# One logarithm for the two heads' units of a key block in a stick-breaking attention, in place of one for each

## What is computed

```python
z = einsum('bhqk', q_blk, kh) * Dh ** -0.5
mask = key_pos < q_pos
log_1m_beta = where(mask, log_sigmoid(-z), 0.0)
between = cumsum(log_1m_beta, reverse=True over keys) - log_1m_beta
weights = where(mask, exp(log_sigmoid(z) + between), 0.0)
out = weights @ v
```

## Time and profile before

| | us |
|---|---|
| median of 3 runs | 1442.71 |
| lowest and highest | 1438.63, 1443.05 |
| the profiled execution's own time | 1436.79 |
| its span, first to last instruction | 1435.1 |

### The profile page before, as it was taken

How to read it: one execution, slowest core, us unless ns; L and a number is a source line. 1 busy time by engine, 2 the same in 40 slices (tenths; PEclk the granted TensorE clock), 3 DMA queues, 4 the chain that set the end, 5 groups by cost and what they waited for, 6 DMA issues and landing times. The chain is left out here.

```text
span 1435.1 us, 27696 instructions
## 1 busy us (share of the span) xinstructions
PE 1358.9 (95%) x11020; PEld 1063.8 (74%) x11020; DVE 871.1 (61%) x1347; ACT 676.8 (47%) x1249; POOL 324.5 (23%) x434
## 2 busy tenths in 40 slices
PE   6999989999999899898999889999999999999997
PEld 5877767777777566555677678888887788888886
DVE  6244261575752465667365787776665656669865
ACT  5533241352423387878354645445443434345541
POOL 6675544542432042435101300000000000000000
PEclk9999999999999799999999999999999999999999
DMA  6555333533225330404242254445444865787952
GB/s 204 145 156 150 103 82 89 149 85 84 62 75 125 122 75 3 90 2 137 89 156 103 81 165 159 142 147 158 157 136 147 279 194 179 257 269 252 305 188 103
DMA packets 191546, 201.07 MB, mean 140 GB/s; under 512 B 36669, under 2 KB 127994, under 8 KB 191418
## 3 DMA queue, kind: packets, MB, share of 16 engines
q1 hardware_dynamic: 145132, 169.47, 37.5%
q10 hardware_dynamic: 46286, 29.84, 7.5%
HBM read 145.06 MB, written 54.20 MB: 139 GB/s over the span
## 5 line engine op out<-in xcount | busy, mean ns | idle before, releaser
L484 POOL TENSOR_TENSOR fr_wL<-fr_raw,fr_wH 128x256 fp32r<-128x256 f32 (+1 forms) x208 | 164.2, 821 | 76.6 <-PE fr_ps_F L1267 54.2
L1267 PE MATMUL fr_ps_F<-fr_hL,fr_wH 128*128 128x512 f32 (+1 forms) x416 | 167.9, 404 | 2.8 <-DVE fr_hL L804 2.4
L1267 PE MATMUL fr_ps_F<-fr_hH,fr_wH 128*128 128x512 f32 (+1 forms) x416 | 166.6, 400 | 0.0
L1267 PE MATMUL fr_ps_F<-fr_hH,fr_wL 128*128 128x512 f32 (+1 forms) x416 | 113.4, 402 | 0.0
L1267 PEld LDWEIGHTS fr_ps_F<-fr_hL,fr_wH 128*128 128x128 f32 (+1 forms) x416 | 76.6, 184 | 22.9 <-issue 3.1
L2618 PE MATMUL all_ps_b<-ro_hH,ro_slot 128*128 128x512 f32 x272 | 88.4, 391 | 3.0 <-ACT pl_p L2120 1.5
L1267 PEld LDWEIGHTS fr_ps_F<-fr_hH,fr_wL 128*128 128x128 f32 (+1 forms) x416 | 76.2, 187 | 20.0 <-issue 3.2
L1267 PEld LDWEIGHTS fr_ps_F<-fr_hH,fr_wH 128*128 128x128 f32 (+1 forms) x416 | 76.8, 185 | 18.8 <-issue 2.3
L478 POOL CAST fr_wH<-fr_raw 128x1024 fp32r<-128x1024 f32 (+1 forms) x42 | 48.5, 1155 | 160.3 <-PE fr_ps_F L1267 140.0
L2627 PE MATMUL all_ps_b<-ro_hH 128*128 128x512 f32 x312 | 75.9, 389 | 0.0
L2627 PE MATMUL all_ps_b<-ro_y 128*128 128x512 f32 x300 | 72.7, 389 | 0.5 <-DVE ro_y L2454 0.5
(11 more groups left out here) (480 smaller groups left out, 3154.9 us busy)
## 6 DMA issues: line engine op xcount, KB each, us to landing
pl_slot<-in_w_ff SPq DMA_DIRECT2D x88, 256.0 KB, 4.4
pl_slot<-second_operands SPq DMA_DIRECT2D x75, 256.0 KB, 3.7
fr_raw<-in_w_in ACTq DMA_DIRECT2D x37, 512.0 KB, 4.2
second_operands<-pl_hL SPq DMA_DIRECT2D x64, 256.0 KB, 2.0
pl_hT<-in_w_ff SPq DMA_DIRECT2D x44, 256.0 KB, 4.5
projected<-fr_stage ACTq DMA_DIRECT2D x39, 256.0 KB, 4.4
pl_hT<-second_operands SPq DMA_DIRECT2D x37, 256.0 KB, 3.8
pl_xt<-in_w_ff SPq DMA_DIRECT2D x16, 512.0 KB, 5.6
```

What stands on the lines that cost most here:

```text
L484: m = pool.tensor_tensor(wL[b][:, k:k + 2, 0:wd], raw[b][:, k:k + 2, 0:wd], wH[b][:, k:k + 2, 0:wd].bitcast(F32), ALU.subtract)
L1267: m = pe.matmul(F[b][0:wd, :], w[b][:, k, 0:wd], a[:, k, :], start=(at_ == 0), stop=(at_ == len(passes) - 1))
```

## The change

The four tiles `E0` to `E3` become one tile `E` of four slots, of the same size in all. `logs(i, u)` still takes the exponential of unit `u`. The logarithm is left out for even units; for odd units one instruction covers two adjoining slots, that of unit `u - 1` and that of `u`. Its semaphore `log` then counts pairs, and `softplus` of both units waits for the same count.

```diff
--- before.py
+++ after.py
@@ -2768,7 +2768,8 @@
         r.sb("early", [P, early.size])
         qd, kd, vp, kS, qH, qL = early.qd, early.kd, early.vp, early.kS, early.qH, early.qL
         vn = r.sb("vn", [P, TB + 1, P])
-        E = [r.sb(f"E{n}", [P, HALF]) for n in range(4)]
+        E_all = r.sb("E", [P, 4, HALF])
+        E = [E_all[:, n, :] for n in range(4)]
         SP = E
         row = [r.sb(f"row{n}", [1, HALF]) for n in range(4)]
         W = [r.sb(f"W{n}", [P, HALF]) for n in range(4)]
@@ -3337,12 +3338,15 @@
                 act.copy(ahead.hH[:, i, :], outT[:]).then_inc(s("m_high"), 1)
 
             def logs(i, u):
+                h, c, b, off, rows, first = UNITS[u]
                 act.wait_ge(s("z"), i * NU + u + 1)
                 if u >= 4 or i:
                     act.wait_ge(s("tri_mm"), i * NU + u - 3)
                 act.activation(part(E[u % 4], u), part(Z[u % NZ], u), ACT.Exp).then_inc(s("exp"), 1)
-                act.wait_ge(s("exp"), i * NU + u + 1)
-                act.activation(part(E[u % 4], u), part(E[u % 4], u), ACT.Ln, bias=1.0).then_inc(s("log"), 1)
+                if h:
+                    act.wait_ge(s("exp"), i * NU + u + 1)
+                    both = E_all[0:rows, u % 4 - 1:u % 4 + 1, off:HALF]
+                    act.activation(both, both, ACT.Ln, bias=1.0).then_inc(s("log"), 1)
 
             def units(i):
                 def weight(u):
@@ -3438,7 +3442,7 @@
 
             def units(i):
                 def softplus(u):
-                    dve.wait_ge(s("log"), i * NU + u + 1)
+                    dve.wait_ge(s("log"), (i * NU + u) // 2 + 1)
                     dve.scalar_tensor_tensor(part(SP[u % 4], u), part(E[u % 4], u), CAP, part(Z[u % NZ], u),
                                              ALU.min, ALU.max).then_inc(s("sp"), 1)
 
```

## The result

| | median us | runs | lowest, highest |
|---|---|---|---|
| before, measured beside it | 1440.13 | 5 | 1438.63, 1443.05 |
| after | 1461.75 | 5 | 1458.83, 1465.31 |

The ratio is 1.0146, with a 95% interval of 1.0122 to 1.0170: the change costs 21.6 us. I had said 1447.5 in a range of 1437 to 1457, so the direction was right and the size wrong.

A forecast was written before the change was run, and what follows sets the result against it. No engine alone was taken to bound `heads`: PE was busiest, but at 61 of 84 units ACT's own queue was the limit. Losses of 8.3 less 3.5 saved gave +4.8 us, 1447.5 us against the median 1442.7, range 1437 to 1457.

The forecast's parts named there:

- the seven steps: Steps between even weights in passes 0, 1 and 2 of `heads` said to be stretched, together +8.3 us.
- The ring over two units: Chain from one even weight through merged logarithm, softplus, POOL and PE to the next: 5.28 to 5.61 us per wide pair.
- The term of pass 2: Units 18 to 26: four wide pairs that took 16.78 us, stretched to 5.4 us a pair, +4.8 us.
- The last step of pass 0: From weight 24 to the sums of unit 26: lengthened by +1.9 us, expected to last.
- The step from pair 6/7 to the wide pair 8/9: First half of passes 0 and 1: chain of 4.79 us against 3.89 and 4.09, so +0.9 and +0.7 us.
- Elsewhere the ring has cover: Wide steps of pass 0, weights 16 to 24, and the end of pass 1: GLA work covers it, 0.25 to 0.6 us spare.
- narrow pairs have shorter rings: Pairs below 512 columns: chain shorter than for wide pairs, so no loss was counted for them.
- the third rival: Wide steps of passes 0 and 1: later softplus delays DVE's GLA pieces; +13.9 us, 1456.6 us; chance 0.13.
- The saving of 3.5 us: ACT's queue: 0.27 us less per pair, counted for 13 pairs taken as truly bound by ACT, -3.5 us.
- thin cover breaks: Eight wide steps of passes 0 and 1 grow 0.7 us each, nothing saved by ACT; 1456.6 us; chance 0.13.
- ACT's queue decides: Logarithm's delay is covered in passes 0 and 1, only ACT's saving counts: -9.5 us, 1433.2 us; chance 0.17.
- both cancel: PE absorbs the stretch of passes 0 and 1, only pass 2 pays: +1.3 us, 1444.0 us; chance 0.32.

The follow-up runs named there:

- split_first: Changed kernel with DVE's split put ahead of the softplus in even units of pass 2; 1467.13 us, one run.
- narrow_first: Kernel before with only pairs below 512 columns merged, and DVE's other work put ahead of the softplus in even narrow units; 1444.84 us, ratio 1.0040.
- merge_narrow: Kernel before with logarithms merged only for pairs below 512 columns; 1448.63 us, ratio 1.0086.
- merge_pass1: Kernel before with logarithms merged in pass 1 only; 1442.27 us, ratio 1.0028.
- after_first: Changed kernel, all pairs merged, with DVE's other work put ahead of the softplus in even narrow units; 1461.47 us, ratio 1.0153.
- both_short: Changed kernel with even units' row copy behind the logarithm on ACT and, in pass 2, DVE's split ahead of the even softplus; 1464.88 us, ratio 1.0180.
- late_two: Changed kernel with two single logarithms, the even one first, behind the odd exponential; each softplus waits for its own; 1452.16 us, ratio 1.0106.
- wait_pair: Kernel before, ACT's queue untouched, but an even unit's softplus also waits for the odd unit's logarithm; 1455.03 us, ratio 1.0126.
- late_rev: Changed kernel with two single logarithms behind the odd exponential, the odd one first, the even softplus waiting for both; 1472.14 us, ratio 1.0227.
- row_last: Changed kernel with the row copy of even units moved behind the logarithms on ACT; 1463.67 us, ratio 1.0170.

## Why the prediction was wrong

Its mechanism of the loss was right and its sum was too small: +4.8 us against +21.6 (25.3 in the trace of after). In that trace the way from 4.8 to 25.3 is: 3.0 more on the seven steps, 3.0 on the eight wide steps of passes 0 and 1 said to have cover, 2.0 on three wide steps that it left out, 8.1 on narrow pairs, 0.9 between the passes, and the 3.5 saved that didn't come.

- **The ring over two units** was right to the instruction, and its size a little small. The two bounds were 5.28 and 5.61, I took 5.4, it was 5.70. ACT's part came as added up (0.96, 0.61, 1.06), POOL's copy was 0.94, the slow value, each time; the handovers to POOL and PE took 0.13 and 0.15 where I had put 0.05 and 0.14. The term of pass 2 was +4.8 and measured 22.79 - 16.78 = **+6.0**.
- **The last step of pass 0**: +1.9, measured +2.7, at a granted clock of 0.85; split_first, with the same order there, took 5.37 us at 1.00, which is +1.9. **The step from pair 6/7 to the wide pair 8/9**: +0.9 and +0.7, measured +1.9 and +0.7. The pair in pass 2, which I left out, grew by 0.8. The seven steps came to 11.3 instead of 8.3.
- **"Elsewhere the ring has cover"** is the step that failed. The steps from weight 16 to 24 of pass 0 went from 23.43 to 25.34 us: the spare 0.25 to 0.6 us wasn't there, since the ring is 5.7 and the four steps aren't equal (6.30, 6.10, 5.84, 5.19). In split_first, at a granted clock of 1.00, the same four took 24.6 us, so 1.2 of the 1.9 are not the clock. Above all, **"narrow pairs have shorter rings"** compared them with the wide ring, not with their own steps. The pair of 390 columns has a ring of 4.94 us where the step was 3.15. The narrow pairs pay 8.1 us in the trace of after, and 10.8 when merged alone; narrow_first shows that about half of it or more comes with the DVE work behind the softplus, part of it queued, part of it beside POOL's copy. I had named this queue, in the third rival, but for wide pairs only.
- **The saving of 3.5 us** isn't to be seen. ACT is 7.7 us less busy, but no group of steps became shorter by more than 0.1 us (single steps of pass 1 moved by -1.0 to +1.7 us). merge_narrow, where I expected at best -2 us, and merge_pass1 are both slower. That a weight's sums were done doesn't show that ACT's queue sets the end. No run here shortens ACT's work without delaying a logarithm, so whether there is anything to save stays open.
- **The rival "thin cover breaks"** was nearest (1456.6, still 5 us short). Its eight steps (weight 16 to 24 of passes 0 and 1) grew by 3.0 us in all, not 5.6, and one of them alone, in pass 1, by 1.7; more came from narrow pairs. "ACT's queue decides" and "both cancel" are refuted by pass 2 alone, +11.3 us at a granted clock of 1.00. The page of the Trainium skill cited for the fixed cost, "VectorE: DVE Perf Modes", section "The TRN2 errata", would have given -7.9 us, an estimate from its figure; ACT's busy time did fall by 7.7, so its figure holds for the engine, and the kernel became 21.6 us slower.
- What was to show it came: wide steps of 5.70 (just above the 5.3 to 5.6 said), ACT idle for 1.4 to 1.6 us before even weights, both waits grown, `back` unchanged. One sign of being wrong came too: three of the eight wide steps of passes 0 and 1 grew by over 0.5 us (1.1, 0.9 and 1.7).

## What to carry to other kernels

Merging two instructions of a software pipeline makes the first one's result wait for the second one's input: sum the ring through the merged instruction for every size of step that occurs, and compare it with that step, the short ones above all. The fixed cost saved (here 7.7 us of ACT's busy time in 42 pairs) didn't show in the time. For each consumer that becomes later, list what stands behind it in its queue and what will then run beside its successor; here that came with about half of what the narrow pairs lost, or more. And when two executions are compared, look at the granted clock of each step first.

## What the runs showed of the hardware

- A one-row copy on POOL of 262 columns takes 0.40 us beside no more than a softplus (after_first at 677.84, narrow_first at 673.59) and 1.32 beside a 1024-column DVE instruction that reads two SBUF tiles (685.38 above); of 512 columns, 0.60 (both_short at 703.85) and 0.94 beside DVE's split (702.52 above).
- A chain over four engines repeats to 0.01 us (5.70, 5.70, 5.70, 5.69; 5.27 four times in late_two). Once the ring had been measured, the wide steps of six edits (late_two, wait_pair, late_rev, row_last, split_first, both_short) came out within 0.02 us of their sums, while the totals of two of them (late_rev, row_last) lay 8 to 9 us above their ranges.
- Two executions of one order agreed to 0.2 us in all where their granted clock was the same, and differed by 5.1 us on eleven steps where it wasn't (after and split_first, up to weight 16 of pass 2).
